# An SSM and convolution block after a mixture-of-experts block: GpSimd's arithmetic in the second block handed to the other engines, operands read from PSUM, work regrouped

## The reference, cut to what matters

```
h = rms_norm(x); proj = h @ w_in
u, z, xbc, dt_raw, gates = split(proj); gates = sigmoid(gates + gate_b)
# convolution branch
v = (val + b) * sigmoid(gt + b);  v = depthwise_conv(v, 31 taps)
conv_out = silu(layer_norm(v)) @ pw_w + pw_b
# SSM branch, 8 groups of 4 heads of 64, state 128
xbc = silu(depthwise_conv(xbc, 4 taps)) -> xs, B, C
y = y_diag + y_off + xs * d_skip;  y = rms_norm_by_group(y * silu(z)) * norm_g
ssm_out = y @ out_w
x = x + rms_norm((g_conv * conv_out + g_ssm * ssm_out) @ w_out)
x = x + rms_norm((silu(h2 @ w_gate) * (h2 @ w_up)) @ w_down),  h2 = rms_norm(x)
```

## Time and profile before

| | us |
|---|---|
| median of 3 runs | 2611.16 (2608.12 to 2615.07) |
| span of the profiled execution | 2608.2 |
| TensorE busy in it | 2164.1 (83%) |
| VectorE busy | 1547.5 (59%) |
| ScalarE busy | 1097.4 (42%) |
| GpSimd busy | 466.8 (18%) |
| mean granted clock of TensorE | 0.868 |

### The profile page before, as it was taken

How to read it: one execution, slowest core, us unless ns; L and a number is a source line. 1 busy time by engine, 2 the same in 40 slices (tenths; PEclk the granted TensorE clock), 3 DMA queues, 4 the chain that set the end, 5 groups by cost and what they waited for, 6 DMA issues and landing times. The chain is left out here.

```text
span 2608.2 us, 25960 instructions
## 1 busy us (share of the span) xinstructions
PE 2164.1 (83%) x10136; PEld 1722.5 (66%) x10136; DVE 1547.5 (59%) x1564; ACT 1097.4 (42%) x1273; POOL 466.8 (18%) x309
## 2 busy tenths in 40 slices
PE   6998976666999999955888777885498976999997
PEld 5885666564666666635777666775377865788786
DVE  4114569347998988834389999999443245233322
ACT  3224542226888888833333344323252223222212
POOL 0002121001222222200344335453100011000000
PEclk9997558767999999975898888997699988999999
DMA  4210000416999999933222122221122221333321
GB/s 143 81 49 1 1 0 1 150 54 225 405 405 404 405 401 399 391 127 113 82 81 65 49 81 81 65 65 49 44 69 81 97 81 33 105 97 97 97 81 65
DMA packets 202066, 346.91 MB, mean 133 GB/s; under 512 B 13871, under 2 KB 149543, under 8 KB 184535
## 3 DMA queue, kind: packets, MB, share of 16 engines
q1 hardware_dynamic: 191280, 332.49, 36.1%
q0 software_dynamic: 5120, 8.40, 1.0%
q10 hardware_dynamic: 5543, 4.34, 0.5%
HBM read 340.93 MB, written 12.65 MB: 136 GB/s over the span
## 5 line engine op out<-in xcount | busy, mean ns | idle before, releaser
L1352 DVE TENSOR_TENSOR wlo_e<-raw_e,whi_e 128x2048 fp32r<-128x2048 f32 x192 | 436.7, 2288 | 64.3 <-ACT whi_e L1284 63.7
L1284 ACT CAST whi_e<-raw_e 128x2048 fp32r<-128x2048 f32 x192 | 366.7, 1912 | 79.0 <-PE pall L1429 36.2
L47 PE MATMUL pall<-hT_hi,w_lo 128*128 128x512 f32 x864 | 355.1, 411 | 52.6 <-DVE yT L2174 33.1
L1639 ACT CAST w_hi<-w_raw 128x2048 fp32r<-128x2048 f32 x89 | 169.5, 1904 | 540.7 <-PE pall L49 540.7
L1647 DVE TENSOR_TENSOR w_lo<-w_raw,w_hi 128x2048 fp32r<-128x2048 f32 x75 | 171.8, 2291 | 352.4 <-ACT w_hi L1639 352.4
L48 PE MATMUL pall<-hT_lo,w_hi 128*128 128x512 f32 x864 | 348.5, 403 | 0.0
L49 PE MATMUL pall<-hT_hi,w_hi 128*128 128x512 f32 x864 | 347.1, 402 | 0.0
L2186 DVE SCALAR_TENSOR_TENSOR mixed<-yT,cols,mixed 128x512 f32<-128x512 f32 x240 | 251.1, 1046 | 7.5
L47 PEld LDWEIGHTS pall<-hT_hi,w_lo 128*128 128x128 f32 x864 | 170.7, 198 | 93.1 <-DVE yT L2174 35.9
L1428 PE MATMUL pall<-whi_e,xs 128*128 128x512 f32 x512 | 210.8, 412 | 9.5 <-DVE wlo_e L1352 4.9
L1429 PE MATMUL pall<-wlo_e,xs 128*64 128x512 f32 x512 | 207.1, 404 | 0.0
(11 more groups left out here) (443 smaller groups left out, 4298.0 us busy)
## 6 DMA issues: line engine op xcount, KB each, us to landing
raw_e<-in_w_expert_up_dram SPq DMA_DIRECT2D x64, 1024.0 KB, 11.1
raw_e<-in_w_expert_down_dram SPq DMA_DIRECT2D x64, 1024.0 KB, 11.7
raw_e<-in_w_expert_gate_dram SPq DMA_DIRECT2D x64, 1024.0 KB, 11.6
w_raw<-in_w_in_dram SPq DMA_DIRECT2D x80, 512.0 KB, 5.2
w_raw<-in_w_gate_up_dram SPq DMA_DIRECT2D x44, 512.0 KB, 5.1
w_raw<-in_w_down_dram SPq DMA_DIRECT2D x22, 512.0 KB, 4.0
mixed<-in_w_in_dram SPq DMA_DIRECT2D x10, 1024.0 KB, 5.0
A<-acs_rows SPq DMA_DIRECT2D x8, 1024.0 KB, 4.8
```

Source lines behind the costliest of these rows:

```text
L47: nc.tensor.matmul(out, w_lo, m_hi, start=start, stop=False)
L1284: nc.scalar.copy(whi[j][:, :], raw[j][:, :]).then_inc(made_hi(e, j)[0], 1)
L1352: nc.vector.tensor_tensor(wlo[j][:, :], raw[j][:, :], whi[j][:, :].bitcast(F32), ALU.subtract).then_inc(made_lo(e, j)[0], 1)
L1639: self.nc.scalar.copy(self.hi[i][:, :], self.raw[i][:, :]).then_inc(self.s_hi, 1)
```

## The change

- Units: the four ssm_gate units come before conv_gate instead of after pw. Their products and sigmoids are made in the last group, into the tiles of `xbc` and `A`, which are kept through `mix`.
- GpSimd: no taps, no `w_lo`, no sums. It makes, per group, two diagonal 128x128 matrices of the skip weights (`dg`). The skip term is eight TensorE products of x with `dg`, in the same accumulation as `yd`.
- SSM taps: ScalarE makes the last tap with bias from the bank (`first_tap`, function Identity); VectorE adds three taps per tile that read the bank itself, two tiles taking turns. `pc`, `tp` and `x_nat` are gone; `xdt` reads the banks; `xbc` has two buffers.
- Depthwise taps: channel tiles in pairs that take turns, so each tap waits for the one two before; 12 before the loop, runs by the list `SPREAD`, 28 behind it. `v` has four buffers.
- The order of ScalarE's list: squares and root, gate, scaling of y and store stand at the front of the next group, before the exponentials. The scaling by the reciprocal moves from VectorE to ScalarE; y is assembled in `outputs`.
- Loads: for the last group the two next units are loaded after A instead of before it.
- `mix`: TensorE's first ssm_out unit waits bank by bank for the product with the gate; the product with the gate, the sum and the low part before w_out take turns on VectorE, and w_out starts on the first tile; the norms work on each row of banks as it is done, without a copy, with VectorE doing the sum; four `xn` buffers; each turned row has banks of its own.

The diff, cut to its core:

```diff
+    at["ssm_gate"] = len(units)
+    units += [columns(w, OFF_GATE + D + 2 * n * P, ...) for n in range(4)]
     at["conv_gate"] = len(units)
...
     @block.sync
-                until = first(n) + 1 if n + 1 < G else LAST + 2
+                until = unit_at["x", n + 1] + 1 if n + 1 < G else SG
                 for u in range(loaded, until):
                     W.load(sp, u)
...
                 sp.dma_start(A..., acs_rows...).then_inc(s["ar"], 16)
+            for u in range(loaded, CG + 2):
+                W.load(sp, u)
...
     @block.gpsimd
+            for n in range(G):
+                if n >= 2:
+                    pool.wait_ge(s["yd"], 2 * (n - 1))
+                for j in range(2):
+                    nc.gpsimd.tensor_scalar(dg[:, n % 2, j, :], ident[:, :], dcol[:, 2 * n + j:2 * n + j + 1], None,
+                                            ALU.mult).then_inc(s["dg"], 1)
...
     @block.scalar
             for n in range(G):
                 more = n + 1 < G
+                if n >= 1:
+                    squares(n - 1)
+                if more:
+                    first_tap(n + 1, 0)
+                if n >= 1:
+                    gate(n)
+                    normed(n - 1)
+                if more:
+                    first_tap(n + 1, 1)
                 if n >= 1:
                     store(n - 1)
+                decays(n)
+                if not more:
+                    ssm_gate(0)
+                W.make_hi(act, ahead(n, 0))
+                b_natural(n)
...
+                    first_tap(n + 1, 2)
+                    first_tap(n + 1, 3)
...
+                W.make_hi(act, ahead(n, 1))
+                if n + 2 < KD:
+                    glu_gate(n + 2)
+                    W.make_hi(act, ahead(n, 2))
+                if more:
+                    silu(n + 1, (0, 1, 2, 3))
+                    W.make_hi(act, ahead(n, 3))
+            squares(G - 1)
+            normed(G - 1)
+            ssm_gate(2)
+            W.make_hi(act, SG + 4)
+            ssm_gate(3)
+            W.make_hi(act, SG + 5)
             store(G - 1)
...
     @block.vector
+            def conv_taps(n, j0):
+                for k in range(PAD):
+                    for j in (j0, j0 + 1):
...
+                        ins = V.scalar_tensor_tensor(dst, banks[j][:, 0:T - lag], col("ssm_w", ...), dst, ALU.mult, ALU.add)
...
+            SPREAD = [(4, 6, 5, 14), (0, 3, 3, 16), (5, 7, 5, 12), (4, 5, 4, 12)] + [(5, 7, 5, 10)] * 3 + [(8, 8, 6, 0)]
             for n in range(G):
+                if n >= 1:
+                    outputs(n - 1)
+                    W.make_lo(dve, ahead(n - 1, 3))
...
+                    root(n - 1)
+                depthwise(spread[0])
                 if more:
+                    conv_taps(n + 1, 0)
+                W.make_lo(dve, ahead(n, 0))
...
+                depthwise(spread[1])
...
+                W.make_lo(dve, ahead(n, 1))
+                depthwise(spread[2])
                 if more:
+                    conv_taps(n + 1, 2)
                 if n + 2 < KD:
+                    glu(n + 2)
+                    W.make_lo(dve, ahead(n, 2))
+                depthwise(spread[3])
+            outputs(G - 1)
+            root(G - 1)
+            W.make_lo(dve, SG + 4)
+            depthwise(8)
+            W.make_lo(dve, SG + 5)
+            depthwise(KD * CONV_K)
...
     @block.tensor
                 if more:
                     unit("x", n + 1)
+                else:
+                    ssm_gate(0)
...
+                        if r % 2 == 0:
+                            mm(banks[4 + c // 2][:, o:o + P], x[:, r // 2, c * P:c * P + P], dg[:, n % 2, r // 2, :], start=True, ...)
...
+                    pe.wait_ge(s["cvb"], 2 * n + 4)
                 for c in range(1, C):
...
+            ssm_gate(2)
             turn_out(G - 1)
+            ssm_gate(3)
```

More of the change, by code:

```diff
@@ L1921, in conv_tile, with places, ahead @@
             return (2 * n + j) if j < 2 else 2 * G + (n if j == 2 else G + n)
[L1923 to L1955, removed]
+        def places(n):
+            if n + 2 < KD:
+                return [unit_at["x", n + 1], unit_at["bc", n + 1], unit_at["glu", n + 2], unit_at["z", n + 1]]
+            if n + 1 < G:
+                return [unit_at["x", n + 1], unit_at["bc", n + 1], None, unit_at["z", n + 1]]
+            return [SG, SG + 1, None, None]
+        def ahead(n, place):
+            u = places(n)[place]
+            return None if u is None else u + 2
         @block.sync
@@ new lines, in silu, with gate @@
+            def silu(n, tiles):
+                for j in tiles:
+                    act.wait_ge(s["cvx"] if j < 2 else s["cvb"], 2 * n + j % 2 + 1)
+                    nc.scalar.activation(xb[n % 2][:, j, :], xb[n % 2][:, j, :], ACT.Silu).then_inc(s["sl"], 1)
+            def gate(n):
+                if n >= 1:
+                    act.wait_ge(s["yt"], n)
+                for j in range(2):
+                    act.wait_ge(W.out, 2 * unit_at["z", n] + j + 1)
+                    nc.scalar.activation(zs[:, 2 * j:2 * j + 2, :], banks[6 + j].rearrange("p (c d) -> p c d", c=2),
+                                         ACT.Silu).then_inc(s["zs"], 1)
@@ L2020, in _, with ssm_gate @@
+            def ssm_gate(u):
+                for j in range(2):
+                    act.wait_ge(W.out, 2 * (SG + u) + j + 1)
+                    nc.scalar.activation(gs[2 * u + j], banks[j], ACT.Sigmoid, bias=col("gate_b", KD + 2 * u + j)).then_inc(s["gt"], 1)
             act.wait_ge(s["dt"], 3)
@@ L2310, in unit, with ssm_gate @@
                         last.then_inc(W.out, 1)
+            def ssm_gate(u):
+                if u == 0:
+                    pe.wait_ge(s["v"], KD)
+                else:
+                    pe.wait_ge(s["gt"], 2 * u)
+                pe.wait_ge(*W.made(SG + u))
+                for j in range(2):
+                    product(nc, pe, W, SG + u, j, banks[j], hT)
             def turn_out(n):
@@ L2421, in mix @@
     mm_nat = g["mixed"]
-    CG, PW, SG, SO, WO, NEXT = (g["unit"][n] for n in ("conv_gate", "pw", "ssm_gate", "ssm_out", "w_out", "gate_up"))
-    s = {n: sem("m_" + n) for n in ("mean mu xc sqd vm rt rstd nrm act gate yh yl pwd gm mx mh ml cp gpo gpr ssq rt2 rs pn x xn "
+    pall = g["pall"]
+    CG, PW, SO, WO, NEXT = (g["unit"][n] for n in ("conv_gate", "pw", "ssm_out", "w_out", "gate_up"))
+    gs = gate_tiles(x0, A)
+    s = {n: sem("m_" + n) for n in ("mean mu xc sqd vm rt rstd nrm act gate yh yl pwo pwd soo wo gm mx mh ml gpo gpr ssq rt2 rs pn x xn "
                                     "tr hi lo").split()}
```

538 lines of the change are left out of this document (247 added, 291 removed).

## The result

Before, the median is 2613.1 us (2608.1 to 2615.9 in four runs); after the change it is **2456.1 us** (2452.4 to 2459.5 in four runs). The ratio is 0.9407, with a 95% interval of 0.9391 to 0.9424. The forecast was 2479, in a range of 2452 to 2522. The profiled execution after took 2453.0, with a span of 2451.3.

What follows compares the result with a forecast made beforehand. VectorE was taken to bound the SSM loop, TensorE nearly all else in the second block. Loop through last groups -68, mix -45, w_out -4, norms -15: total -132, median 2479 us, range 2452 to 2522.

Steps and rivals of the forecast that it cites:

- rival (b): Loop and last groups: late load hurts less, -10, and TensorE keeps full clock at 57, -10: 2459 us; chance 0.12.
- Stretching, 12 us a group: SSM loop: VectorE's taps run longer beside GpSimd, 12 us of each group, which the change removes.
- VectorE's group, 51: SSM loop: VectorE's busy time a group falls from 69.1 to 51 us.
- Pairs, 0.12 a tap: VectorE's taps taken in turn from two tiles: 0.66 us each against 0.78 for dependent ones, -4.7 a group.
- TensorE's group: SSM loop: TensorE's pieces sum to 56 us; period 57, plus two for clock lost after short waits: 59.
- In front of the loop, +4: Before the loop: glu(0) now waits for six taps behind w_lo on VectorE, costing 4 us.
- Last two groups, 57.1 and 94.5: Loop's end: late state-gate load makes group 6 57.1 us; from there to the next stage's TensorE start, 94.5.
- Mix, -45: Second block's mix: four gate units leave, 54.1 us; a 6.2 wait and 2.9 for low clock come in: -45.
- w_out, -4: Before w_out: TensorE starts 7.5 us earlier but is fed at 1.86 us for four steps: -4 us.
- (a): SSM loop: pairs bring nothing and VectorE stays the bound, 65 us a group, 2514 us in all; chance 0.20.
- (c): SSM loop: without rests TensorE is granted half speed, its 56 us a group become 112: 2745 us; chance 0.03.
- (d): SSM loop: waits only renamed, an overlooked dependency keeps 75 us a group: 2582 us; chance 0.03.

Runs made afterwards that it cites:

- e_reads: Kernel after the change, with GpSimd given 24 multiplications a group on its own scratch tile that nobody waits for: 2514.6 us.
- e_writes: Kernel after the change, with GpSimd given 60 memsets a group on its own scratch tile that nobody waits for: 2458.4 us.
- e_skip: Kernel after the change, without TensorE's eight skip-term products by the diagonal a group: 2445.1 us.
- e_store: Kernel after the change, with ScalarE's evacuations of the transposed y moved back behind the exponentials: 2491.2 us.
- e_load: Kernel after the change, with the first two state-gate units loaded before the last group's A transfer instead of behind it: 2449.8 us.
- e_spread: Kernel after the change, with seven more depthwise taps in each of groups 4, 5 and 6 instead of at the end: 2450.2 us.

## Why the prediction was right, and where its sizes were off

The direction and the mechanism held: VectorE's group shrank below TensorE's, TensorE became the bound, and the four gate units moved. The sum missed by 25 us: forecast -132, measured -157 on the profiled spans. Of these, 11.8 lie in the five steady groups, 4.4 in the last two, 3.6 in front of x(2) and 2.8 at w_out. By its number the result, 2456, is nearer to rival (b)'s 2459 than to the forecast of 2479, and it is 4 us inside the range. Two signs that were named fell just outside: a period of 57 to 61 (56.64), and 15 to 20 us of taps behind the last gate unit (13.3). Step by step:

- **Stretching, 12 us a group.** The cause is right, by e_reads and e_writes. The mechanism is sharper than "beside GpSimd": it takes a reading GpSimd instruction and two SBUF operands. The size was taken from means over the whole kernel; in the five steady groups the means before are 1037 and 1782 ns, which, less 0.78 for each of 34 and 6 taps, makes an estimated 15 us a group.
- **VectorE's group, 51.** Measured 49.5 in the last steady group and 46 to 51 in the others, 48.8 on average.
- **Pairs, 0.12 a tap.** Right (0.786 and 0.663). A tap from a bank at 0.66: right, six in 4.02.
- **TensorE's group, "56", then "two more for clock lost after short waits: 59".** The sum of the pieces was right, 55.7 busy; the skip term was priced at 2.1, e_skip measured 1.8. **The step that failed is the two us for the clock**; the other 0.36 is rounding 55.9 and 0.8 of waiting up to 57. The only wait, 0.81 us in front of the turned y, left the granted clock at 1.00. Five groups at 2.36 less are 11.8 us, half of the miss. A wait of 0.8 cost nothing behind it here; e_store shows what the allowance would have fitted: 1.6 us for a wait of 3.4.
- **Waits go.** Right: 0.81 before the turned y where 0.8 was forecast; none for `yT` (e_store: 3.4 a group without the move).
- **In front of the loop, +4.** The wait grew from 6.1 to 10.3, as forecast. From the start of `groups` to x(1) the profiles show only 1.7 more, 95.3 for 93.6, because the small products before the wait (96 of 32 columns) happened to run at a granted clock of 0.68 and not 0.57, and took 15.2 us instead of 18.1. Over all profiles the stretch is 89.9 to 93.6 in the three of the kernel before and its variants, and 93.7 to 95.3 in the others.
- **Last two groups, 57.1 and 94.5.** The late load is as described: 7.1 us of wait at `yo` of group 6 where 10 were forecast (the unit landed 8.5 us behind A's issue, not 10), then the 20 taps and 23 us with TensorE idle. Group 6 took 55.2 for 57.1, the tail 92.0 for 94.5. e_load and e_spread show that both are real costs and could be had back. Rival (b) had joined "the load hurts less, -10" with full clock, -10; only its second half came true as written; the unit landed at t 41.7 of group 6, between the forecast's 44 and its 39. So its 2459, close to the 2456 measured, is in part luck.
- **Mix, -45, and norms, -15.** -45.2 and -15.0. The gap before ssm_out is 6.26 where 6.2 was forecast. **w_out, -4:** measured -6.8. The start came 7.5 us earlier as forecast; the slow feed had been charged for four steps, but TensorE starts at the lower clock, where one step took 1.7 to 1.8, about as long as three VectorE instructions (1.80), and only 0.15 and 0.83 were lost in two waits.
- **Rivals (a), (c) and (d).** The period is 56.64 and not (a)'s 65 or (d)'s 75. For (c), the clock went up, not down: 1.00 in every steady group.
- **GpSimd's two diagonals a group, put at 0.** Right: they took 1.9 to 3.5 us together, and of the taps beside them one took 0.85 instead of 0.75.

What was not tried: the move of the four gate units, the norms by tile and the interleaving before w_out were not undone one by one, nor were the taps' reading from banks and the `w_lo` taken from GpSimd. What each is worth is read from the traces alone.

## What to carry to other kernels

Price an engine that "only helps" by what it does to its neighbour: count GpSimd instructions that read SBUF, and VectorE instructions with two SBUF operands or at double rate, and keep them apart in time, or feed VectorE from a bank. When the bound moves to another engine, look at the first and last rounds of the loop again: here 23.5 us of the loop were still to be had there, in a load issued behind a wait and in twenty instructions left for the end. A reordering that removes a wait can cost 20 us or more on one side of such a shift and bring 31 on the other, so don't price it by the wait's own total.

## What was not expected of the hardware

- VectorE and GpSimd alternate instruction by instruction: a 0.66 us tap takes on the 1.45 us pitch of its neighbour, and a 0.54 us one waited 4.3 us for a single 128x2048 instruction of GpSimd.
- A one-operand instruction at double rate is slowed by GpSimd's pure writes too (1227 to 1456 ns), while the two-operand taps are not (748 and 749).
- A rest of 0.8 us in each 56.6 us left TensorE at its full 2.4 GHz through five groups, while in e_store one of 3.4 more, a few products later, lowered the group's clock to 0.97.
